# A second place in SBUF for expert weights, and loads that run two chunks ahead, in a fused two-block network

## What is computed

```python
def moe_swiglu(xn, w_router, w_gate, w_up, w_down):        # 8 experts, top 2, hidden width 3584
    logits = (xt @ w_router)
    top_vals, top_idx = lax.top_k(logits, TOP_K)
    top_w = jax.nn.softmax(top_vals, axis=-1)
    combine = sum(one_hot(top_idx) * top_w)
    for e in range(N_EXPERTS):
        y = y + combine[:, e:e + 1] * swiglu(xt, w_gate[e], w_up[e], w_down[e])
# swiglu(x, g, u, d) = (silu(x @ g) * (x @ u)) @ d
```

## Time and profile before

| what | us |
|---|---|
| median of 3 runs | 2860.66 |
| lowest, highest | 2859.99, 2863.47 |
| the profiled execution, device time | 2862.23 |
| its span in the trace | 2860.5 |
| the stage of the experts in it, first L1738 to last L1717 | 859.6 |

### The profile page before, as it was taken

One profiled execution on the slowest core, in us unless ns is written; L12 is line 12 of the kernel. 1 busy time (PEld: TensorE's weight loads), 2 busy tenths in 40 slices (PEclk: granted clock), 3 DMA queues, 4 the chain that ended last, 5 costly groups with the idle time before them and its releaser, 6 DMA issues. The chain is left out here.

```text
span 2860.5 us, 76137 instructions
## 1 busy us (share of the span) xinstructions
PE 2653.4 (93%) x34649; PEld 2200.0 (77%) x34649; DVE 673.8 (24%) x1724; ACT 430.1 (15%) x1039; POOL 88.0 (3%) x168
## 2 busy tenths in 40 slices
PE   8899999989989999999999999899989789878998
PEld 7677777768779999989989978666667577766664
DVE  5411000271120110110110111400043576752001
ACT  1111000110110110100110111400012344431000
POOL 0100000010000000000000000000000000010000
PEclk9899999989989999999999999999999798889999
DMA  7334443534339999999999993374541000002442
GB/s 223 113 130 133 132 153 126 166 118 135 145 116 404 407 408 407 407 407 407 407 408 407 407 366 103 98 221 155 173 131 56 5 7 7 4 4 96 148 160 88
DMA packets 290526, 571.23 MB, mean 200 GB/s; under 512 B 18326, under 2 KB 181141, under 8 KB 290405
## 3 DMA queue, kind: packets, MB, share of 16 engines
q1 hardware_dynamic: 290404, 569.49, 55.0%
HBM read 568.37 MB, written 5.28 MB: 201 GB/s over the span
## 5 line engine op out<-in xcount | busy, mean ns | idle before, releaser
L1738 PE MATMUL ps<-xg,ring 128*64 128x80 f32 x14336 | 517.3, 234 | 8.3 <-issue 3.0
L1738 PEld LDWEIGHTS ps<-xg,ring 128*64 128x64 f32 x14336 | 504.3, 137 | 19.4 <-DMA ring<-in_moe_w_up_dram 9.3
L1333 PE MATMUL ps<-xT,ring 128*128 128x256 f32 x1728 | 379.8, 379 | 4.7 <-PEq L452 3.1
L1333 PEld LDWEIGHTS ps<-xT,ring 128*128 128x128 f32 x1728 | 328.0, 190 | 65.9 <-issue 22.4
L1345 PE MATMUL ps<-ring,hidden 128*128 128x512 f32 x688 | 301.8, 592 | 0.0
L1754 PE MATMUL ps<-hidden,expert_down 128*64 128x80 f32 x7168 | 260.0, 233 | 9.7 <-DVE hidden L1830 5.7
L1754 PEld LDWEIGHTS ps<-hidden,expert_down 128*64 128x64 f32 x7168 | 251.9, 137 | 15.7 <-DVE hidden L1830 7.6
L1345 PEld LDWEIGHTS ps<-ring,hidden 128*128 128x128 f32 x688 | 130.7, 190 | 147.5 <-issue 145.4
L618 PE MATMUL ps<-ring,xT 128*128 128x256 f32 (+1 forms) x1056 | 228.2, 379 | 7.5 <-PEq L1214 3.9
L618 PEld LDWEIGHTS ps<-ring,xT 128*128 128x128 f32 x1056 | 198.3, 195 | 36.1 <-issue 9.3
L618 PE MATMUL ps<-xT,ring 128*128 128x256 f32 (+1 forms) x944 | 214.4, 389 | 10.2 <-PEq L596 4.5
(11 more groups left out here) (380 smaller groups left out, 2482.6 us busy)
## 6 DMA issues: line engine op xcount, KB each, us to landing
ring<-in_moe_w_gate_dram SPq DMA_DIRECT2D x128, 896.0 KB, 16.4
ring<-in_moe_w_up_dram SPq DMA_DIRECT2D x128, 896.0 KB, 16.7
expert_down<-in_moe_w_down_dram SPq DMA_DIRECT2D x96, 1024.0 KB, 17.0
ring<-in_mlp_w_dram SPq DMA_DIRECT2D x64, 1024.0 KB, 5.4
ring<-in_w_xkv_dram SPq DMA_DIRECT2D x16, 1024.0 KB, 5.3
expert_down<-in_moe_w_down_dram SPq DMA_DIRECT2D x32, 512.0 KB, 16.5
ring<-in_ffn_w_gate_dram SPq DMA_DIRECT2D x11, 1024.0 KB, 5.3
ring<-in_ffn_w_up_dram SPq DMA_DIRECT2D x11, 1024.0 KB, 5.3
```

The source lines that it names most:

```text
L1333: mm = pe.matmul(bank[:, m * SEQ:(m + 1) * SEQ], w[:, c, m * P:(m + 1) * P], self.xT[:, c, :], start=(c == 0), stop=(c == KC - 1))
L1738: mm = pe.matmul(bank[b][o:o + HEAD, at, :], w[:, c, f * P + o:f * P + o + HEAD], xg[:, p * E_STEP + c, :], start=(p == 0 and c == 0 and a ...
```

## The change

- `memory`, `memory_g` and `memory_rows` become parts of one tile `second` of 56 KB a partition, as does the scratch of the norms and of the attention output (`spare_rows`), and three small tiles of `bias_rows`. Gate and up pieces get their second place in it (`par` 1).
- Ahead of the stage, `expert_ahead_gate` now also loads the four gate pieces and two up pieces of the second chunk, `expert_ahead_up` the other two up pieces.
- SP's loads are written out for the first three items: gate and up of chunk g+2, then down of chunk g+1, for 8 chunks; from there, and in the loop over later items, gate, up and down of one chunk after another, where gate and up wait for the chunk two before.
- PE's inner loop runs over pairs of chunks (`n // 2`), and its body holds two chunks, one for each place.
- Some semaphores are merged or dropped.

```diff
-    def expert_in(self, kind, p):
-        slot = (6 + E_PIECES * kind + p) % RING
-        return self.ring[:, slot, 0:E_STEP * E_WIDE].rearrange("p (c f) -> p c f", c=E_STEP)
+    def expert_in(self, kind, p, par):
+        if par:
+            at = (E_PIECES * (1 - kind) + p) * E_STEP * E_WIDE
+            flat = self.second[:, at:at + E_STEP * E_WIDE]
+        else:
+            flat = self.ring[:, (6 + E_PIECES * kind + p) % RING, 0:E_STEP * E_WIDE]
+        return flat.rearrange("p (c f) -> p c f", c=E_STEP)
...
     def expert_ahead_gate(self, sp):
...
+        for p in range(E_PIECES):
+            self.load_expert_in(sp, 0, p, 1, slice(0, 1), second)
+        for p in range(2):
+            self.load_expert_in(sp, 1, p, 1, slice(0, 1), second)
...
     def expert_ahead_up(self, sp):
...
+        for p in range(2, E_PIECES):
+            self.load_expert_in(sp, 1, p, 1, slice(0, 1), second)
...
+                for g in range(2 * n):
+                    load_in_early(g + 2)
+                    load_out_early(g + 1)
+                load_out_early(2 * n + 1)
+                for g in range(2 * n + 2, 3 * n):
+                    load_in_early(g)
+                    load_out_early(g)
+                with sp.Fori(3, count) as i:
+                    e = bass.ds(sp.value_load(items_e[0:1, bass.ds(i, 1)], min_val=0, max_val=E - 1), 1)
+                    for k in range(n):
+                        load_in(e, k, k % 2, lambda p: i * (n * E_PIECES) + ((k - 2) * E_PIECES + p))
+                        load_out(e, k, lambda p: i * (n * downs) + ((k - 1) * downs + p))
...
                 with pe.Fori(0, count) as i:
-                    with pe.Fori(0, n) as k:
-                        g = i * n + k
+                    def chunk(g, nth, par):
...
+                    with pe.Fori(0, n // 2) as k:
+                        for par in range(2):
+                            chunk(i * n + k * 2 + par, i * (n // 2) + k, par)
```

More of the change, by code:

```diff
@@ L217, in __init__ @@
         self.mlp = self.mlp_signals("ffn_")
+        self.mlp["loaded"] = [[sem(f"ffn_{kind}{p}_loaded") for p in range(2)] for kind in ("gate", "up", "down")]
         self.moe = self.mlp_signals("moe_")
@@ L224, in __init__ @@
         self.y_copied = [sem(f"moe_y_copied{half}") for half in range(2)]
-        self.expert_loaded = [[sem(f"expert_{kind}{p}_loaded") for p in range(E_PIECES)] for kind in ("gate", "up", "down")]
+        self.expert_loaded = [[[sem(f"expert_{kind}{p}_{par}_loaded") for p in range(E_PIECES)] for par in range(2 if kind != "down" else 1)]
+                              for kind in ("gate", "up", "down")]
         self.yT_ready = sem("moe_yT_ready")
@@ L290, in constants @@
             put(3 + i // 2, [f"conv_a{l}{i}" for l in layers], I["conv_a_w"][:, :, i * P:(i + 1) * P].rearrange("l k p -> (l k) p"))
-        x_loaded, step, cols_turned, cols_ready = (self.sig(n) for n in ("x_loaded", "constants_step", "cols_turned", "cols_ready"))
+        x_loaded, step, cols_turned = (self.sig(n) for n in ("x_loaded", "constants_step", "cols_turned"))
         with ExitStack() as ctx:
@@ L350, in constants @@
             self.side_loaded.over(16 * loads)
-            step.over(4)
+            step.over(6)
             cols_turned.over(1)
-            cols_ready.over(2)
             for signal, n in ((self.squares_summed, TT), (self.pool_step, TT), (self.rstd_ready, TT), (self.rows_scaled, TT), (self.turned, KC)):
@@ L500, in close_and_norm, with norm_beside @@
             self.turned.over(KC)
-    def norm_beside(self, ctx, src, dst, gain, jobs, load=None, scaled_too=None):
+    def norm_beside(self, ctx, src, dst, gain, jobs, load=None, scaled_too=None, rows=None):
         junk = self.tmp(ctx, "junk", [P, D])
-        rows = self.tmp(ctx, "rows", [P, TT, D])
+        rows = self.tmp(ctx, "rows", [P, TT, D]) if rows is None else rows
         stat = self.tmp(ctx, "stat", [P, 3, TT])
@@ L1252, in cross_attention @@
             with ExitStack() as inner:
-                work, close = self.norm_beside(inner, self.h, self.xT, f"norm_x_g{l}", 8)
+                work, close = self.norm_beside(inner, self.h, self.xT, f"norm_x_g{l}", 8, rows=self.spare_rows)
                 self.add_rows(memory_g, 256, v, add=False, beside=work)
@@ L1661, in expert_items @@
         zeros_ready = self.sig("moe_zeros_ready").sem
-        loaded = [[x.sem for x in xs] for xs in self.expert_loaded]
+        loaded = [[[x.sem for x in xs] for xs in places] for places in self.expert_loaded]
         ADDS = 2 * TT
@@ L1673, in _, with load_in @@
                 count = items(sp)
-                def load(e, free, k):
-                    cols = slice(0, E_WIDE) if k is None else bass.ds(k * E_WIDE, E_WIDE)
+                def load_in(e, k, par, free):
                     for kind, done in ((0, gate_done), (1, up_done)):
                         for p in range(E_PIECES):
-                            sp.wait_ge(done, free(E_PIECES, p + 1))
-                            self.load_expert_in(sp, kind, p, e, cols)
+                            sp.wait_ge(done, free(p + 1))
+                            self.load_expert_in(sp, kind, p, par, e, slice(k * E_WIDE, (k + 1) * E_WIDE))
@@ L1682, in load, with load_out @@
+                def load_out(e, k, free):
                     for p in range(downs):
[L1683 to L1696, removed]
+                        at = k * FB + sum(E_DOWN[:p])
+                        sp.wait_ge(down_done, free(p + 1))
@@ new lines, in load_out, with load_in_early, load_out_early @@
+                        self.load_expert_out(sp, p, e, slice(at, at + E_DOWN[p]))
+                def load_in_early(g):
+                    load_in(of_item[g // n], g % n, g % 2, lambda p: (g - 2) * E_PIECES + p)
+                def load_out_early(g):
+                    load_out(of_item[g // n], g % n, lambda p: (g - 1) * downs + p)
+                of_item = []
+                for i in range(3):
+                    e = sp.value_load(items_e[0:1, i:i + 1], min_val=0, max_val=E - 1)
+                    of_item.append(bass.ds(e, 1))
@@ L1889, in bias_rows @@
         table = self.tmp(ctx, "table", [32, H])
-        of_bucket = self.tmp(ctx, "of_bucket", [32, DIST])
-        mask = self.tmp(ctx, "mask", [H, DIST])
-        line = self.tmp(ctx, "line", [H, DIST])
+        of_bucket, mask, line = (self.second[0:rows, 3 * UNIT + n * DIST:3 * UNIT + (n + 1) * DIST] for n, rows in enumerate((32, H, H)))
         sums = self.ps[0:H, 7, :]
@@ L2929, in network @@
         with ExitStack() as inner:
-            memory, memory_g = (m.tmp(inner, n, [P, KC, SEQ]) for n in ("memory", "memory_g"))
-            memory_rows = m.tmp(inner, "memory_rows", [P, TT, D])
+            m.second = m.tmp(inner, "second", [P, 2 * E_PIECES * E_STEP * E_WIDE])
+            memory, memory_g = (m.second[:, n * UNIT:(n + 1) * UNIT].rearrange("p (c s) -> p c s", c=KC) for n in range(2))
+            memory_rows = m.spare_rows = m.second[:, 2 * UNIT:3 * UNIT].rearrange("p (t e) -> p t e", t=TT)
             m.constants()
```

33 lines of the change are left out of this document (17 added, 16 removed).

## The result

| | us |
|---|---|
| before, median of 4 runs beside it | 2862.06 (2859.99 to 2865.16) |
| changed, median of 4 runs | 3121.86 (3119.18 to 3130.33) |
| ratio, with its 95% interval | 1.0914 (1.0893 to 1.0934) |
| span of the profiled execution, before and after | 2860.5, 3128.6 |
| stage of the experts in it, before and after | 859.6, 1128.3 |

The changed kernel is 9% slower. The profiled execution of the changed kernel was the slowest of its four, 8.5 us above their median. The two spans differ by 268.1 us, the stages by 268.7: all of it lies in the stage of the experts. Ahead of it the profiled execution is 5.0 us late (845.9 for 840.9), and behind it 5.6 us are given back.

The account below looks back on a forecast made before the run. The experts' stage was taken as bound by DMA, PE 40 us behind; refetching PE's doubled loop makes eight items 1103 us against 859.6, +244, with the 18 us of loads ahead not coming off: 3105 us, range 2925 to 3240.

Parts of the forecast that it names:

- The bound before: Experts' stage, 859.6 us: bound by DMA at 108.1 us an item, PE needing 102.4.
- Part 1: Eight pieces loaded ahead of the experts' stage: cost nothing, gain 18.0 us as long as DMA is the bound.
- Part 2: Order and places of the experts' loads: no byte changes, nothing to gain, no place where SP holds it up.
- Part 3: PE's doubled loop body, 11.5 blocks of 256 instructions: doesn't stay in the engine, is fetched again throughout; stage +244 us.
- The sum: Experts' stage: an item takes 25 block times + 7.9 us, 137.9 us; eight items 1103 against 859.6.
- The time of a block: Fetching one block of 256 PE instructions in the experts' loop: 5.2 us, three quarters at 5.48, one at 4.43.
- upper bound of 6.2: Top value for one block's fetch, mean of the two late first-pass blocks (6.95 and 5.48 us): 163 us an item.
- The pauses of DMA: Experts' stage: DMA busy only 108 of 145 us, so blocks asked for while engines are free come in time.
- The jumps: PE's jumps back in the experts' loops: each costs a full block time, one a pass plus one to the outer loop.
- 12 B - 0.7: One PE pass of two chunks: 12 times B, the time for one block, less 0.7 us hidden by queued work.
- The doubled loop stays: Rival: PE's doubled experts' loop stays in the engine, loads ahead decide, stage 841.6 us, time 2843; 15%.
- part of the loop stays: Rival: some 8 of 11.5 blocks of PE's doubled loop are kept, an item 117 us, time 2937; 8%.

Follow-up runs that it names:

- half_after: The changed kernel with half of the experts' matmuls left out, all loads kept: 2846.65 us, ratio 0.9945 to the kernel before.
- small matmuls: The kernel before with 28, 36, 48, 96 or 160 tiny zero-adding matmuls ending each item's tail: 2874.72, 2945.71, 2952.55, 3031.85, 3139.06 us.
- double_body: The kernel before with only PE's chunk loop body doubled to two chunks, no second place or loads ahead: 3112.59 us, ratio 1.0882.
- four_body: The kernel before with PE's chunk loop written out fully, four chunks in a row: 3068.31 us, ratio 1.0727.

## Why the prediction was right, point by point

The forecast was 3105 us in 2925 to 3240; measured were 3121.86.

**The bound before** held. With PE's work halved the kernel before takes 2856.1 us, 0.14% less: it was bound by DMA, with PE 5 us an item behind.

**Part 1** was right in kind. The gain in the stage is 20.0 us where PE is no bound, and nothing where it is. Wrong was "cost nothing": I priced SP's loads by the first four of a burst (0.6 us); behind the eight that were there already the next four took 2.4 us each, and SP then came late to a point where all engines meet. At full work that is 2.2 us, and in `half_after` 2.0 us with 3.9 more for the lower clock behind it. The price came from issuing these loads right ahead of such a point, not from their bytes.

**Part 2** held: half_after shows no loss by order or places.

**Part 3** held in its mechanism: q8 packets through the whole stage (200, for 180 to 200 expected), halts every 256 instructions, DMA share 0.80 (0.8), 303 GB/s (320), items of 141.0 us (137.9). The capacity, which no row of before could show, was measured by the small matmuls: 8 blocks of 256 instructions. It is what the Trainium skill, page "Runtime: NRT & Kernel Launch", section "Instruction fetch mechanics", states with 2048 instructions. The block asked for ahead takes one of the 8, so here a loop could touch only 7.

**The sum** was right by errors that cancel. *The time of a block* was put at 5.2 us. Taken over the stage, the 75 blocks that begin and end with a halt took 6.05 us in the mean (4.8 to 7.6), nearer to the upper bound of 6.2 than to my value. They are the late ones; blocks with a shorter wait or none stand beside them. With the 12 blocks that the sum gives a pass, the measured passes come to 5.6 us a block. The 0.7 us a pass for work queued in PE is shown by no run. *The pauses of DMA* didn't help as I had reckoned: the share is 0.80, but over the two passes above it is 0.90 and 0.91, and much of the free time lies behind the jumps (0.02 over the first 4 us of the item, below). *The jumps* I counted three an item; there are two, one within the item and one to the next. A pass took 66.6 and 65.4 us, not the 61.7 of 12 B - 0.7, and the third jump's 5.2 us fell away: 137.9 + 2 x 4.3 - 5.2 = 141.3, against 141.0. That the item came within about 3 us of the forecast is luck in part: a pass cost more than I had put, and a jump that isn't there made up for more than half of it. *The clock* was missing. The granted clock was 0.93 over the stage, where it had been 1.00:

```profile
987.04:991.00 3.96, 3.54 (x62) 3.55 (x64) 0.00 (x0) 0.00 (x0) 0.00 (x0) 0.57 0.02 4
991.00:995.00 4.00, 4.00 (x122) 4.00 (x118) 0.00 (x0) 0.00 (x0) 0.00 (x0) 1.00 0.68 202
...
1038.30:1042.00 3.70, 3.70 (x66) 3.70 (x64) 0.41 (x1) 0.00 (x0) 0.00 (x0) 0.55 0.80 262
```

In these rows PE runs for some 3.5 us at the lower of its two levels, 1.2 GHz, behind a halt of 3.1 us (to 987.46) and one of 2.9 (to 1036.92): half as many matmuls in the same time (66 in 3.70 us against 122 in 4.00). Behind the halts of 1.6 us above the clock stays at 1.00. In between it is one way or the other: 0.57 behind the 2.11 us that end at 894.52, but 1.00 behind 2.51 us that end at 865.62, and 1.00 behind the 2.23 us of the earlier trace rows, as the earlier trace rows show. Of the 38.6 us that an item lost against PE's own 102.4, the halts named "issue" are (206.4 + 23.4) / 8 = 28.7; in the table of waits of the changed kernel (us, count, longest):

```profile
PE ps L1760 <- issue: 206.4, 102, 7.1
...
PE ps L1776 <- issue: 23.4, 26, 2.1
```

The other 9.9 are not halts, and the clock is what is left to explain them: 141 us at 0.94 are short of full speed by 8.5. That last step is argued, not shown by a run of its own. With four chunks in the body, and halts of mostly 1.0 to 1.9 us in a row, the clock was 0.98 in the item shown, and 0.97 over the stage, where double_body had 0.94. So much of the 44 us between them is clock (some 35 us, an estimate: 6% of double_body's stage of 1112 us less 3% of four_body's 1067), and "5.5 us a jump" has it in it.

**The rivals.** "The doubled loop stays", at 15%, and "part of the loop stays", at 8%, are both out: in the doubled loop every block is fetched in every pass (25 an item, for two passes of 10.5 blocks, the tail and what is fetched past the jumps). The reason given against the second, that a loop run in order drives out what it needs next, is what the runs with small matmuls show.

## What to carry to other kernels

Count the instructions of a hardware loop on PE before you unroll it. A float32 matmul is four instructions; here a loop stayed up to 7 blocks of 256 (1642 instructions) and cost a fetch for every block from 1674 on. In these traces the sign is an instruction queue that goes on carrying packets inside a loop, and PE halts "issue" at a fixed distance of 256 instructions; the first pass of the kernel before had such halts, and the loop that didn't stay had them in each pass. Loads ahead pay only where DMA stays the bound. Here they win 20 us in the stage at best, and whatever comes with them may cost PE no more than its margin of 5 us an item.

## What the runs showed of the hardware that was not expected

- One block over the room costs all blocks of the loop: from 6 packets in the stage to 69, and 71 us for 32 instructions, of which the small matmuls themselves may be 13.
- Halts of 2.9 us and more brought the granted clock down in the item shown: 0.55 to 0.57 for some 3.5 us behind them, 0.93 over the stage. Of those of 2.1 to 2.5 us some did and some didn't.
- At a jump back, two blocks are fetched together. Two q8 packets moved between 907 and 910 us, at the jump for which PE halted from 905.5 to 912.4, longer than the 5.48 us of one block in the earlier trace rows.
- SP's issue of a DMA took 0.6 us with an empty queue and 2.4 us with some 8 loads of 0.9 MB in it (an estimate from their 18.2 us to landing, at 407 GB/s).
- A float32 MATMUL instruction of 128 columns by 80 takes 115 ns with its weight load, one of 64 columns 34: two halves are much cheaper than a whole.
- A small matmul, 64 columns of one row by 8, costs 0.16 to 0.21 us in the program (four instructions, in part at the lower clock), more than twice the 0.07 us of one of 64 columns and 128 rows by 80.
